# Prompt attention: three score banks in a ring by chunk and head, four banks of transposed probabilities, one bank for the outputs of two units

## The reference

```
logits = q k^T * scale + bias          (bias holds the mask too)
probs  = exp(logits - max), denominator = sum(probs)
out    = gate * (probs v) / denominator
```

## Time and profile before

| | |
|---|---|
| median of 3 runs | 2533.96 us (2529.08 to 2538.34) |
| profiled execution | 2529.99 us |
| its span, first to last instruction | 2528.2 us |
| mean granted TensorE clock | 0.945 |
| busy in the span | PE 2280.5, DVE 968.5, ACT 578.2, POOL 464.9 us |
| prompt attention | about 1074 to 1508 us of the span |

### The profile page before, as it was taken

One profiled execution on the slowest core, in us unless ns is written; L12 is line 12 of the kernel. 1 busy time (PEld: TensorE's weight loads), 2 busy tenths in 40 slices (PEclk: granted clock), 3 DMA queues, 4 the chain that ended last, 5 costly groups with the idle time before them and its releaser, 6 DMA issues. The chain is left out here.

```text
span 2528.2 us, 34780 instructions
## 1 busy us (share of the span) xinstructions
PE 2280.5 (90%) x13808; PEld 1477.6 (58%) x13808; DVE 968.5 (38%) x2332; ACT 578.2 (23%) x1255; POOL 464.9 (18%) x664
## 2 busy tenths in 40 slices
PE   7999998999594689388888879999999999999998
PEld 3445666666362366255555554488888888844443
DVE  3001003333131354155555542267767675600110
ACT  3000002333121243155555541111111010100110
POOL 1313212221100355000121210013223322100000
PEclk9999998999787799799999899999999999999999
DMA  7712116775665789432123303156565642510110
GB/s 240 215 73 76 45 40 237 273 284 190 233 233 164 252 360 405 149 103 74 46 76 105 97 31 95 58 164 234 200 218 200 217 147 71 178 56 1 60 36 17
DMA packets 165878, 376.31 MB, mean 149 GB/s; under 512 B 47846, under 2 KB 104526, under 8 KB 147887
## 3 DMA queue, kind: packets, MB, share of 16 engines
q1 hardware_dynamic: 131964, 148.68, 18.8%
q0 software_dynamic: 25216, 149.43, 15.4%
q10 hardware_dynamic: 8538, 75.99, 8.7%
HBM read 345.71 MB, written 99.65 MB: 176 GB/s over the span
## 5 line engine op out<-in xcount | busy, mean ns | idle before, releaser
L2629 PE MATMUL ff_ps<-ff_hx,ff_aw 128*128 128x264 f32 x2464 | 552.8, 387 | 0.9 <-DVE ff_hx L2868 0.9
L2629 PEld LDWEIGHTS ff_ps<-ff_hx,ff_aw 128*128 128x128 f32 x2464 | 469.1, 191 | 81.6 <-issue 1.2
L337 PE MATMUL in_ps<-in_w,in_xT 128*128 128x512 f32 (+1 forms) x512 | 199.6, 545 | 0.0
L659 PE MATMUL pa_psT<-pa_ident,pa_L 128*128 128x128 f32 x816 | 129.4, 295 | 57.0 <-DVE pa_PT L817 46.9
L761 ACT ACTIVATE pa_L<-pa_L,pa_nm 128x128 f32<-128x128 f32 (+3 forms) x192 | 141.7, 740 | 84.9 <-DVE pa_nm L801 84.6
L791 DVE CUSTOM_DVE_ANT_0 pa_L<-pa_psS,pa_T 128x512 f32<-128x512 f32 (+3 forms) x288 | 138.3, 530 | 48.8 <-PE pa_psS L641 48.8
L659 PEld LDWEIGHTS pa_psT<-pa_ident,pa_L 128*128 128x128 f32 x816 | 92.0, 147 | 110.8 <-DVE pa_PT L817 52.6
L641 PE MATMUL pa_psS<-pa_kT,pa_qT 64*128 64x512 f32 (+3 forms) x576 | 122.8, 533 | 36.4 <-POOL pa_qT L708 35.6
L337 PEld LDWEIGHTS in_ps<-in_w,in_xT 128*128 128x128 f32 x512 | 95.2, 190 | 93.6 <-issue 84.9
L459 DVE TENSOR_SCALAR in_yout<-in_ps 128x512 f32<-128x512 f32 (+2 forms) x44 | 26.1, 593 | 300.3 <-PE in_ps L337 190.9
L1034 DVE COPY cmp_KT<-cmp_psT 128x512 f32<-128x512 f32 x128 | 88.5, 692 | 96.3 <-PE cmp_psT L950 96.3
(11 more groups left out here) (380 smaller groups left out, 3012.4 us busy)
## 6 DMA issues: line engine op xcount, KB each, us to landing
out_new_a_k_s<-in_cache_a_k ACTq DMA_DIRECT2D x8, 4088.0 KB
out_new_a_v_s<-in_cache_a_v ACTq DMA_DIRECT2D x8, 4088.0 KB
ff_aw<-in_w_up SPq DMA_DIRECT2D x44, 512.0 KB, 15.7
in_w<-in_w_in SPq DMA_DIRECT2D x5, 2048.0 KB
cd_X<-in_cache_a_k SPq DMA_DIRECT2D x8, 1024.0 KB
cd_X<-in_cache_a_v SPq DMA_DIRECT2D x8, 1024.0 KB
ff_hx<-in_w_down SPq DMA_DIRECT2D x14, 512.0 KB, 4.4
cd_X<-in_cache_a_k SPq DMA_DIRECT2D x24, 256.0 KB
```

The lines of the kernel that those rows point to most:

```text
L337: mm = pe.matmul(ps[0:n, b, 0:width], xT[:, k, t * P:t * P + n], w[:, ch % WBUF, k, 0:width], start=(k == 0), stop=(k == KC - 1))
L659: mm = pe.transpose(psT[:, b % 2, (x - x0) * P:(x - x0) * P + P], L[:, u % 3, h, j * P:j * P + P], ident[:, :])
L2629: mm = pe.matmul(ps[:, bank_of(x, j, g), 0:H2], aw[:, j % 2, at, k, :], hx[:, bt, k, g * H2:g * H2 + H2], start=(k == 0), stop=(k == KH - 1))
```

## The change

`psS` has three banks. A chunk and head has the number q = 2c + h and the bank q modulo 3, and each matmul waits for the logits of q - 3. `psT` has four banks, and a transpose waits for the copy of the bank four earlier. `psO` has one bank of 2 x 256 values, so `values(u)` now waits for `finish(u - 1)`. The gates go into the unit's own 256 values; the sigmoid is moved to the front of ScalarE's step 11, ahead of the copies, and TensorE waits for it ahead of the values of unit 8 itself.

```diff
--- before.py
+++ after.py
@@ -553,9 +553,9 @@
         rgB = m.sb("rgB", [P, 4, 2, HD])
         tmp = m.sb("tmp", [P, 4, P])
         Rs = m.sb("Rs", [P, 4, P])
-        psS = m.ps("psS", [P, 2, 2, 512])
-        psT = m.ps("psT", [P, 2, 512])
-        psO = m.ps("psO", [P, 2, 512])
+        psS = m.ps("psS", [P, 3, 512])
+        psT = m.ps("psT", [P, 4, 512])
+        psO = m.ps("psO", [P, 2, 2 * P])
         s_id = m.sem("identity_loaded")
         s_gl = m.sem("gates_loaded")
         s_mc = m.sem("compressed_rows_loaded")
@@ -634,11 +634,12 @@
                 for c in range(chunk0[u], chunk0[u + 1]):
                     k0 = (c - chunk0[u]) * 512
                     w = min(512, nk * P - k0)
-                    if c >= 2:
-                        pe.wait_ge(s_lg, 2 * (c - 1))
                     for h in range(2):
                         r = slice(h * HD, h * HD + HD)
-                        pe.matmul(psS[:, c % 2, h, 0:w], qT[r, i, qt * P:qt * P + P],
+                        q = 2 * c + h
+                        if q >= 3:
+                            pe.wait_ge(s_lg, q - 2)
+                        pe.matmul(psS[:, q % 3, 0:w], qT[r, i, qt * P:qt * P + P],
                                   kT[r, i, j0 * P + k0:j0 * P + k0 + w], start=True, stop=True).then_inc(s_qk, 1)
 
             def transposes(u):
@@ -647,16 +648,16 @@
                     pe.wait_ge(s_id, 16)
                 pe.wait_ge(s_ex, 2 * (u + 1))
                 for b in range(bank0[u], bank0[u + 1]):
-                    if b >= 2:
-                        na, nd = copied(b - 1)
-                        if on_dve(b - 2):
+                    if b >= 4:
+                        na, nd = copied(b - 3)
+                        if on_dve(b - 4):
                             pe.wait_ge(s_cd, nd)
                         else:
                             pe.wait_ge(s_ca, na)
                     x0 = 4 * (b - bank0[u])
                     for x in range(x0, min(x0 + 4, 2 * nk)):
                         j, h = x // 2, x % 2
-                        mm = pe.transpose(psT[:, b % 2, (x - x0) * P:(x - x0) * P + P],
+                        mm = pe.transpose(psT[:, b % 4, (x - x0) * P:(x - x0) * P + P],
                                           L[:, u % 3, h, j * P:j * P + P], ident[:, :])
                     mm.then_inc(s_tr, 1)
 
@@ -667,13 +668,12 @@
                 pe.wait_ge(s_ca, na)
                 if nd:
                     pe.wait_ge(s_cd, nd)
-                if u >= 2:
-                    pe.wait_ge(s_wt, u - 1)
+                if u:
+                    pe.wait_ge(s_wt, u)
                 if u == QT:
                     pe.wait_ge(s_gl, 32)
-                    pe.matmul(psO[:, u % 2, 2 * P:2 * P + QT * 24], flip[:, :],
+                    pe.matmul(psO[:, u % 2, 0:QT * 24], flip[:, :],
                               gates[:, :, :].rearrange("p t n -> p (t n)"), start=True, stop=True).then_inc(s_gf, 1)
-                if u == QT + 2:
                     pe.wait_ge(s_gs, 1)
                 for j in range(nk):
                     for h in range(2):
@@ -741,6 +741,10 @@
         @block.scalar
         def _(act):
             for s in range(U + 3):
+                if s == QT + 3:
+                    act.wait_ge(s_gf, 1)
+                    nc.scalar.activation(gsig[:, :, :], psO[:, QT % 2, 0:QT * 24].rearrange("p (t n) -> p t n", t=QT),
+                                         ACT.Sigmoid).then_inc(s_gs, 1)
                 if 2 <= s < U + 2:
                     u = s - 2
                     nk = parts(u)[5]
@@ -752,7 +756,7 @@
                         x0 = 4 * (b - bank0[u]) * P
                         w = min(512, 2 * nk * P - x0)
                         act.wait_ge(s_tr, b + 1)
-                        nc.scalar.activation(PT[:, u % 3, x0:x0 + w], psT[:, b % 2, 0:w], ACT.Copy).then_inc(s_ca, 1)
+                        nc.scalar.activation(PT[:, u % 3, x0:x0 + w], psT[:, b % 4, 0:w], ACT.Copy).then_inc(s_ca, 1)
                 if s < U:
                     w = parts(s)[5] * P
                     act.wait_ge(s_nm, s + 1)
@@ -765,10 +769,6 @@
                     act.wait_ge(s_pv, 3 * (u + 1))
                     if u >= 4:
                         act.wait_ge(s_wt, u - 3)
-                    if u == QT:
-                        act.wait_ge(s_gf, 1)
-                        nc.scalar.activation(gsig[:, :, :], psO[:, u % 2, 2 * P:2 * P + QT * 24].rearrange("p (t n) -> p t n", t=QT),
-                                             ACT.Sigmoid).then_inc(s_gs, 1)
                     nc.scalar.activation(Rs[:, u % 4, :], psO[:, u % 2, P:2 * P], ACT.Copy).then_inc(s_rs, 1)
 
         @block.vector
@@ -788,7 +788,7 @@
                     n = min(512, w - 512 * x)
                     dve.wait_ge(s_qk, 2 * (c + 1))
                     for h in range(2):
-                        dve.tensor_tensor_reduce(L[:, u % 3, h, 512 * x:512 * x + n], psS[:, c % 2, h, 0:n],
+                        dve.tensor_tensor_reduce(L[:, u % 3, h, 512 * x:512 * x + n], psS[:, (2 * c + h) % 3, 0:n],
                                                  T[:, it % 2, h, SEQ - w + 512 * x:SEQ - w + 512 * x + n], 1.0, NEG,
                                                  ALU.add, ALU.max, mx[:, u, h, x:x + 1]).then_inc(s_lg, 1)
                 dve.wait_ge(s_lg, 2 * chunk0[u + 1])
@@ -814,7 +814,7 @@
                     if u >= 3:
                         dve.wait_ge(s_pv, 3 * (u - 2))
                     dve.wait_ge(s_tr, b + 1)
-                    dve.tensor_copy(PT[:, u % 3, x0:x0 + w], psT[:, b % 2, 0:w]).then_inc(s_cd, 1)
+                    dve.tensor_copy(PT[:, u % 3, x0:x0 + w], psT[:, b % 4, 0:w]).then_inc(s_cd, 1)
 
             def finish(u):
                 it, ki, p, qt, j0, nk = parts(u)
```

## The result

The changed kernel takes 2541.69 us (median of 20 runs, 2533.62 to 2551.65); the kernel before, in 20 runs beside it, 2536.15 us. The ratio is 1.0027 with a 95% interval of 1.0014 to 1.0040: slower by some 7 us. I had forecast 4 us faster. The time lies inside the range given, 2506 to 2553 us, but the direction is wrong: the whole interval of the ratio lies above 1.

The account below looks back on a forecast made before the run. It took the attention stage's loop of `finish`, logits, maximum, exponentials and `Rs` as the bound. Terms +1.5 + 1.1 - 5.3 - 1.4 = -4.1 us against the median of 2533.96 gave 2529.9, called 2530; range 2506 to 2553.

Parts of the forecast that it names:

- part 2: Three score banks: a big unit's fourth score waits for its first logits operation; transposes start at L+1.06 to L+1.38 us.
- step 3: Attention step, `finish` to `finish`, numbered modulo 8; 7 key blocks (1, 5, 7: 8, 6, 5); 6.87 us, before 7.05.
- L: Start of a step's logits on VectorE, from which times in us count; step 3 transposes from L+1.27.
- E: When ScalarE's exponentials can start, counted from L; by the copies 3.44, 3.83 or 3.88 us in step 3.
- step 1: Attention step with 8 key blocks; forecast 6.84 us, before 6.43.
- The 48 steps: Attention steps from 1157.67 to 1374.08 us, 216.4 us before; forecast 217.9, +1.5.
- Iterations of five blocks: The 24 attention steps from 1374.08 to 1476.66 us; 32.42 us instead of 34.19 per eight steps, -5.3 altogether.
- Last eight: The last eight attention steps, up to the drain; estimated at some -1.4 us.
- Part 3: Outputs of two units in one bank: values start 0.35 us after `finish`; one even step is longer, by 0.36 us.
- Part 4: Gates' sigmoid ahead of ScalarE's copies, so ScalarE waits for TensorE; once, +1.1 us, between 0 and +2.5.
- The clock: TensorE's clock in the attention stage: waits below 1 us each were assumed to leave it high, near 1.00.
- the waits: Rival: in the attention stage two new waits cost 0.2 us more per odd step, 48 times: +10, 2540 us; chance 0.12.

Follow-up runs that it names:

- the pair run: Changed kernel with the third score matmul also waiting for the first logits operation, so it goes with the fourth; ratio to the kernel before 1.0039.
- the version with four score banks: Kernel before with three transposed banks instead of two, one shared output bank, four score banks kept, sigmoid moved; 2500.15 us, ratio 0.9860.
- only the ring: Kernel before with `psS` in three banks by chunk and head, `psT` and `psO` as before; ratio 1.0088.
- the split order: Changed kernel with two banks of transposes ahead of the second chunk of scores; 2519.91 us, ratio to the kernel before 0.9940.

## Why the prediction was wrong

The loop, the places of both new waits and the end of the long one were right. What failed is one term of part 2: "Eight passes at 512 columns took 1.91 us to the first transpose, so 0.2 + 0.2135 each." The division assumed that the eight passes run one after another. They don't, and so each column of the lone fourth score was taken at half its price. The kernel before shows it when TensorE's timeline is asked in narrow windows, the first at the beginning of the eight passes, the second at their end:

```profile
1183.48 0.70 PE L641 MATMUL pa_psS<-pa_kT,pa_qT 64*128 64x512 f32 x2
```

```profile
1184.44 1.02 PE L641 MATMUL pa_psS<-pa_kT,pa_qT 64*128 64x512 f32 x4
```

Two passes together last no longer than 0.70 us: the two heads, on rows 0 to 63 and 64 to 127, start side by side. The last four last 1.02; with 0.59 for one matmul of this width (593 ns at L2588 in the page of the kernel before), the starts of two pairs are 0.43 us apart. So a pass of 512 columns costs 0.43 us, which a second head shares for nothing, and the 1.91 us are 0.2 + 4 x 0.43. The Trainium skill says as much: in "TensorE: Matmul & The Clock Gate", the part on packing small matmuls, weight loads and matmuls on different row groups overlap. The trace agrees, 0.43 us for two. A fourth score alone then costs twice what I took, and two runs show it: with its columns cut to 128, step 3 fell by 0.42 us, where the price of the prediction had 0.21; and sent together with the third (the pair run), it left all steps as they were.

Point by point, in us against the profiled stage (predicted, measured):

- Fourth score to the transposes, 384 columns: L+1.27, measured L+1.60 in the step 3 shown above. The 0.75 us until it starts was right (0.76). The second chunk's logits come 0.47 late (1214.17, where 1213.70 was possible), not 0.30. Both are the same term. In that step the exponentials start 4.14 us behind the logits (1212.47 to 1216.61), where I had E at 3.88; the other terms of the step are right within 0.05.
- Step 3 at 6.87 in that order of banks, measured 7.21, the mean of its two; step 5 6.25, measured 6.44; step 7 4.93, measured 5.05; step 1 6.84, measured 7.12. Eight steps 36.5, measured 37.6 where all are of 8 to 5 blocks. The 48 steps: +1.5, measured +8.1.
- Iterations of five blocks: -5.3, measured -3.5 (33.01 for 32.42 expected). The fourth score is 128 columns wide there, so it errs least. Last eight: -1.4, measured -1.0.
- Part 3: step 0 at 2.48, measured 2.57. Values start 0.44 us after `finish`, not 0.35, which is these 0.09 us:

```profile
1199.54 0.29 DVE L829 TENSOR_TENSOR ffn_G<-pa_psO,pa_Rs 128x128 f32<-128x128 f32 x1 [2.01 <-ACT pa_Rs L772]
...
1199.98 1.53 PE L681 MATMUL pa_psO<-pa_PT,pa_V 128*64 128x128 f32 x24 [0.37 <-DVE ffn_G L829]
```

Alone, with two transposed banks, the shared output bank cost 12 us, a case that is not in the sum.
- Part 4, the gates: +1.1 taken, at most 2.5. Step 11 of the kernel took 10.07 us (8.21 before) and step 12 4.47 (3.27): +3.1. ScalarE's first table load was hidden in its wait, but the exponentials then needed theirs too, behind the copies:

```profile
1131.74 1.28 ACT L746 ACT_TABLE_LOAD   x1
1136.36 0.33 ACT L746 ACTIVATE pa_gsig<-pa_psO 128x192 f32<-128x192 f32 x1 [3.34 <-PE pa_psO L675]
...
1138.18 1.28 ACT L765 ACT_TABLE_LOAD   x1
```

The 3.1 us are a ceiling for the gates. Step 12 lies in a stretch at a granted clock of 0.50 (1142.8 to 1146.1 us), and in the version with four score banks, which moves the gates too and has no such stretch there, the two steps take 12.10 us against 11.48 before. Step 11 also grew where only the ring was there, to 8.86.
- The clock: right in what came of it. The 12 slow stretches are gone, by step times where they had cost most (step 0 of the short iterations 3.64 before, 2.36 after). The assumption, waits below 1 us each, did not hold: the longest TensorE wait behind 1170 us is 1.36. The rule of the Trainium skill that the prediction names, dense work keeps the clock high, agrees. The length of one wait does not decide it: before, the 12 stretches stood behind waits of 1.61 to 2.21 us, while waits of 2.38 and 2.58 brought none; with the split order three slow stretches stand behind waits of 2.17 us and four more such waits have none behind them; and the version with four score banks has nine waits of 1.75 to 2.00 us and a clock of 1.00 from 1078 us to its last `finish`. What decides it stays open.
- What the sum left out: the start. It has no term for the first 15 units but the gates. From the first scores to the first `finish` the stage took 15.3 us before and 19.9 after, and to the `finish` of unit 14 81.0 and 90.0: +9.0 us. Two iterations' worth of the pass price, 2.1 us, belong there, and at most 3.1 are the gates' own. The rest may in part be the clock of this one execution. It is low for the first 3.8 us of the stage before, and for the first 16.8 us after:

```profile
1074.20:1077.90 3.70, 3.70 (x12) 1.52 (x12) 1.90 (x8) 0.88 (x4) 0.00 (x0) 0.50 1.04 384
1078.00:1089.40 11.40, 8.45 (x61) 4.75 (x61) 5.94 (x26) 7.51 (x17) 0.88 (x3) 1.00 0.67 219
...
1081.60:1098.30 16.70, 15.91 (x42) 8.41 (x42) 8.26 (x34) 5.59 (x15) 0.87 (x3) 0.50 0.70 232
```

Over all ten profiles, the time to the first `finish` is 13.2 to 17.0 us in the six in which the low level lasts 3 to 7 us from the first scores, and 17.8 to 19.9 in the four in which it lasts 15 to 18. Two of the six have the ring (15.7 and 17.0 us), all of the four have it, so that the ring's own share at the start is not separated.

The stage measured by these terms is +4.6 +4.4 +8.1 -3.5 -1.0 = +12.6 us in the profiled pair (the first two are the start). The medians differ by 5.5 and the ratio says 6.9. Which part of the stage differs in other executions stays open, since a profile shows only one; but this one took 5.5 us more than the median of its kernel.

With the pass at 0.43 us the transposes of steps 3, 5, 7 and the logits of step 1 come 0.32, 0.21, 0.11 and 0.43 us later than in my sum, 1.07 per iteration, 8.6 in eight of them, and 4 x 0.11 in each of the four short ones, 1.8. The same sum would have given -4.1 + 10.3 = +6.2 us, where the medians have +5.5. Behind the start it would have been right within 0.5 us by parts: +7.6 for the 48 steps (measured +8.1), -4.0 for the iterations of five blocks (-3.5), -1.1 for the last eight (-1.0). At the start it would have had +3.4, measured +9.0. So this one term turns the sum from faster to slower by itself. The missing term for the start is the second fault of the sum; in the profiled pair it is worth as much, and that the corrected total still comes so near the medians may be luck.

Of the rivals, "the waits" came nearest in time: 0.2 us more in each odd step, 2540. Its reason was near too, since the wait of the fourth score cost more than taken, though not by a wait that ended later but by a matmul that lasted longer. Neither of the two signs that the prediction named for being wrong appeared, a step 3 below 6 us or a low clock that stays: both watched the gain, and none the price of the ring.

## What to carry to other kernels

Before a bank is taken from a ring, see which instruction then waits and what stands behind it in the same engine's order: here a score matmul of 0.4 to 0.9 us held back 2.0 us of transposes. A third bank for these was worth 48 us beside four score banks, while a fourth, bought with a score bank, was worth less than it cost (ratio 1.0027 against 0.9860). A duration worked out by dividing a merged row by its count is only right if the members run one after another; ask the timeline for one or two of them. Where an engine must wait anyway, put independent work into the wait: transposes ahead of the waiting score took some 22 us off the changed kernel, and scores ahead of the waiting values some 13 off the version with four score banks, by the ratios to before.

## What was unexpected of the hardware

The two heads' fp32 score passes run side by side on the two halves of the rows, 0.43 us per pass of 512 columns for the pair, and a head alone takes as long per column (0.82 ns by the cut-down score). Two waits of TensorE of 2.58 us left the clock high, others of 1.61 and 1.65 us were followed by the lower level, and all 12 such stretches went when no wait was over 1.36 us, with TensorE's work unchanged. They also went in a version that has waits of 1.75 to 2.00 us.
